# Moving the step sizes and decays of a state-space mixer into the layer ahead of it

## What is computed

```python
proj = h @ w_in                                  # 1024 -> 2048 (z) + 3072 (xbc) + 32 (dt)
xbc = silu(causal_dwconv(xbc, conv_w, conv_b))   # 4 taps
dt = softplus(dt_raw + dt_bias)                  # 32 heads x 256 tokens
a = -exp(a_log)
# ssd_chunked, 2 chunks of 128 tokens, 4 groups of 8 heads, head 64, state 128
a_cs = cumsum(dt * a)                            # inside each chunk
xdt = x * dt
decay = exp(a_cs[l] - a_cs[s]) for s <= l
y_diag = ((C B^T) * decay) @ xdt
states = B^T @ (exp(a_cs[last] - a_cs) * xdt)    # chunk 0 hands its state to chunk 1
y_off  = (C @ states) * exp(a_cs)
y = (y_diag + y_off + x * d_skip) * silu(z)
y = grouped_rms_norm(y) ; out = y @ w_out
```

## Time and profile before

| what | value |
|---|---|
| median of three runs | 1482.74 us (1481.03 to 1485.03) |
| profiled execution, its own time | 1484.64 us |
| its span in the trace | 1482.9 us |
| mean granted clock of TensorE | 0.964 of full speed |
| busy: TensorE, VectorE, ScalarE, GpSimd | 93%, 70%, 51%, 10% of the span |
| TensorE's share of the chain that ended last | 71% |

### The profile page before, as it was taken

One profiled execution on the slowest core, in us unless ns is written; L12 is line 12 of the kernel. 1 busy time (PEld: TensorE's weight loads), 2 busy tenths in 40 slices (PEclk: granted clock), 3 DMA queues, 4 the chain that ended last, 5 costly groups with the idle time before them and its releaser, 6 DMA issues.

```text
span 1482.9 us, 30231 instructions
## 1 busy us (share of the span) xinstructions
PE 1381.3 (93%) x12445; PEld 1325.4 (89%) x12445; DVE 1040.0 (70%) x1688; ACT 761.6 (51%) x1257; POOL 141.5 (10%) x147
## 2 busy tenths in 40 slices
PE   7998999997798999999997599999999998899997
PEld 6997988896798999999995499999999887899997
DVE  5769898986676656557696877887555655678843
ACT  5594483326645444354563855544454455554432
POOL 2000000000101111001002102211010100222100
PEclk9999999997999999999999699999999999999999
DMA  8533510210262665645445344554655521455550
GB/s 267 171 113 114 172 56 2 88 60 30 92 194 86 205 191 165 198 149 160 154 135 153 114 154 158 172 174 148 219 171 175 196 85 59 157 185 170 180 190 29
DMA packets 204338, 211.05 MB, mean 142 GB/s; under 512 B 8579, under 2 KB 201867, under 8 KB 204059
## 3 DMA queue, kind: packets, MB, share of 16 engines
q1 hardware_dynamic: 202154, 200.87, 42.7%
q0 software_dynamic: 1968, 8.44, 2.0%
q10 hardware_dynamic: 96, 0.02, 0.0%
HBM read 207.70 MB, written 1.62 MB: 141 GB/s over the span
## 4 chain that ended last, share of the span: by engine, by line
PE 71%; DVE 16%; ACT 5%; issue 4%; DMA 2%; POOL 1%; SPq 0%; DVEq 0%; ACTq 0%; POOLq 0%
PE pb L417 19%; PE pb L419 19%; PE pb L418 19%; DVE w_lo L446 2%; DVE pj L1453 2%; PE pb L1937 1%; DVE sub L1381 1%; PE pb L403 1%; PE pb L2307 1%; DVE x_lo L1229 1%; PE pb L1979 1%; PE pb L1926 1%; ACT w_hi L440 1%; DVE sub L1382 1%; PE pb L1932 1%
## 5 line engine op out<-in xcount | busy, mean ns | idle before, releaser
L446 DVE TENSOR_TENSOR w_lo<-raw,w_hi 128x1024 fp32r<-128x1024 f32 (+1 forms) x384 | 471.3, 1230 | 161.1 <-ACT w_hi L440 160.5
L417 PE MATMUL pb<-x_hi,w_hi 128*128 128x256 f32 x1968 | 564.2, 287 | 19.8 <-DVE w_lo L446 10.1
L440 ACT ACTIVATE w_hi<-raw 128x1024 fp32r<-128x1024 f32 (+1 forms) x384 | 395.5, 1042 | 340.9 <-PE pb L419 298.9
L418 PE MATMUL pb<-x_lo,w_hi 128*128 128x256 f32 x1968 | 559.9, 284 | 0.0
L419 PE MATMUL pb<-x_hi,w_lo 128*128 128x256 f32 x1968 | 559.8, 284 | 0.0
L417 PEld LDWEIGHTS pb<-x_hi,w_hi 128*128 128x128 f32 x1968 | 381.1, 194 | 24.7 <-DVE w_lo L446 15.9
L418 PEld LDWEIGHTS pb<-x_lo,w_hi 128*128 128x128 f32 x1968 | 381.0, 194 | 0.3
L419 PEld LDWEIGHTS pb<-x_hi,w_lo 128*128 128x128 f32 x1968 | 380.8, 193 | 0.0
L417 PE MATMUL pb<-act_hi,w_hi 128*128 128x256 f32 x528 | 149.5, 283 | 1.1 <-DVE w_lo L446 1.1
L418 PE MATMUL pb<-act_lo,w_hi 128*128 128x256 f32 x528 | 149.4, 283 | 0.0
L419 PE MATMUL pb<-act_hi,w_lo 128*128 128x256 f32 x528 | 149.4, 283 | 0.0
(11 more groups left out here) (312 smaller groups left out, 2103.2 us busy)
## 6 DMA issues: line engine op xcount, KB each, us to landing
raw<-in_ffn_w_up_dram SPq DMA_DIRECT2D x55, 1024.0 KB, 5.1
raw<-in_w_in_dram SPq DMA_DIRECT2D x28, 1024.0 KB, 5.1
raw<-in_ffn_w_down_dram SPq DMA_DIRECT2D x24, 896.0 KB, 4.8
raw<-in_ssd_w_in_dram SPq DMA_DIRECT2D x20, 1024.0 KB, 5.3
raw<-in_fox_w_in_dram SPq DMA_DIRECT2D x16, 1024.0 KB, 5.8
raw<-in_ffn_w_down_dram SPq DMA_DIRECT2D x12, 1024.0 KB, 5.3
raw<-in_ffn_w_gate_dram SPq DMA_DIRECT2D x11, 1024.0 KB, 5.3
raw<-in_ssd_w_out_dram SPq DMA_DIRECT2D x8, 1024.0 KB, 6.3
```

The lines of the kernel that those rows point to most:

```text
L417: pe.matmul(o, w_hi[m][:, k, :], hi[:, k0 + k, :], start=first and k == 0, stop=False)
L418: pe.matmul(o, w_hi[m][:, k, :], lo[:, k0 + k, :], start=False, stop=False)
L440: act.activation(w_hi[m][:, 0:nk, :], raw[s][:, 0:nk, m * P:(m + 1) * P], ACT.Copy).then_inc(sem("w_hi_ready"), 1)
L446: dve.tensor_tensor(w_lo[m][:, 0:nk, :], raw[s][:, 0:nk, m * P:(m + 1) * P], w_hi[m][:, 0:nk, :].bitcast(F32), ALU.subtract).then_inc(sem( ...
```

## The change

- **Step sizes early.** The 32 step-size columns (`dt_w`, 128 KB) are no longer a layer. SyncE loads them ahead of `down0`, after a wait for the last `w_lo` of `up0`. TensorE does `narrow_product` between `ssd_z` and `ssd_xbc`. VectorE and ScalarE do the step sizes and decays behind block (0, 1) of `ssd_xbc`; ScalarE loads the table of Ln and Exp there, and that of SiLU again before the first `xbc_sigmoids`.
- **Decays broadcast early.** GpSimd sends `acs` out at that point and fetches six `att` pieces at once (i = 0 to 5), then writes exp(acs) of chunk 1, 32x128, to DRAM and broadcasts it as `eab`, which now lies in the chunk 1 half of `y_ssd` and needs no exponential afterwards.
- **Scaled x on VectorE.** `xdt_end` is made in four pieces of 128x512 on VectorE, between the pieces of `xdt` of chunk 1, instead of one 128x2048 on GpSimd. It lies where `x_lo` was, and `b_tok` where `x_hi` was.
- **Four units ahead of the states.** Units 0 to 3 run before the chunk states and y_off (`chunk_states`, called at i = `FIRST_UNITS` = 4 on TensorE and VectorE). The skip terms move from i = 0..7 to i = 4..11, the `ssd_out` splits on VectorE from i = 4..6 to i = 9..11; ScalarE's three heads for `ssd_out` move into the last unit of `ssd_xbc`.

The core of the diff:

```diff
+        x_lo_plain = nc.alloc_sbuf_tensor_at("x_lo_plain", [P, KC * T], F32, offset=x_hi_base + KC * T * 4)
+        xdt_end = x_lo_plain[:, :]
+        NATT, FIRST_UNITS = 6, 4
...
+        eab = y_ssd[:, :, P:T]
+        dt_w = pj[:, 90, :].rearrange("p (k n) -> p k n", n=SSD_HEADS)
+        acs_exp = small[:, P:T]
+        b_tok = x_hi_plain[:, 0:512].rearrange("p (g n) -> p g n", g=SSD_GROUPS)
...
-        layer("ssd_dt", narrow(a["ssd_w_in_2"][0], 5120, SSD_HEADS), [KC], dmas=(1, 0))
...
+                if ly.name == "down0":
+                    sp.wait_ge(sem("w_lo_ready"), L["up0"].item1)
+                    sp.dma_start(dt_w, a["ssd_w_in_2"][0].rearrange("(k p) n -> p k n", p=P)[:, :, 5120:5120 + SSD_HEADS]).then_inc(sem("dt_w_loaded"), 16)
...
             pool.wait_ge(sem("sub_dma"), ACS_OUT)
-            pool.wait_ge(sem("xbc_ready"), SSD_XBC)
+            for i in range(NATT):
+                decay_piece(i)
+            pool.wait_ge(sem("da_ready"), 1)
+            pool.dma_start(acs_dram[2], acs_exp).then_inc(sem("sub_dma"), 16)
+            pool.wait_ge(sem("sub_dma"), ACS_OUT + 16)
             for h in range(2):
-                src = acs_dram[1].rearrange("(a m t) l -> t a m l", a=1, t=2)[h]
+                src = acs_dram[2].rearrange("(a m t) l -> t a m l", a=1, t=2)[h]
                 pool.dma_start(eab[64 * h:64 * h + 64, :, :], src.broadcast_to([64, SSD_Z, P])).then_inc(sem("sub_dma"), 16)
-            for i in range(2):
-                decay_piece(i)
-            pool.wait_ge(sem("xdt_ready"), 4)
-            pool.tensor_tensor(xdt_end.rearrange("p (h d) -> p h d", d=HEAD),
-                               xdt[:, 0, :].rearrange("p (h d) -> p h d", d=HEAD),
-                               tok_heads[:, 4, :].unsqueeze(2).broadcast_to([P, SSD_HEADS, HEAD]), ALU.mult).then_inc(sem("xdt_end_ready"), 1)
-            pool.wait_ge(sem("st_done"), SSD_GROUPS)
-            for i in range(2, 16):
-                if i >= NATT:
-                    pool.wait_ge(sem("y_done"), i - NATT + 1)
+            for i in range(NATT, 16):
+                pool.wait_ge(sem("y_done"), i - NATT + 1)
...
+                if isinstance(u, int) and (u, m) == (0, 1):
+                    step_sizes()
+
+            def step_sizes():
+
+                log_exp()
+                act.wait_ge(sem("small_loaded"), 16 * 12)
+                go(act.activation(heads_col[:, 3:4], heads_col[:, 1:2], ACT.Exp))
+                act.wait_ge(sem("abs_ready"), 1)
+                link(act.activation(dt_e, dt_e, ACT.Exp, scale=-1.0))
+                act.activation(dt_e, dt_e, ACT.Ln, bias=1.0).then_inc(sem("log_ready"), 1)
+                act.wait_ge(sem("acs_ready"), 2)
+                act.activation(acs_exp, acs[:, P:T], ACT.Exp)
+                act.activation(da_end, acs[:, 0:P], ACT.Exp, scale=-1.0, bias=acs[:, P - 1:P]).then_inc(sem("da_ready"), 1)
...
-            act_layer(act, L["ssd_xbc"], xbc_hook, lead=2)
+            act_layer(act, L["ssd_xbc"], xbc_hook, lead=2, nxt=L["ssd_out"])
...
-            ahead(act_head, act, L["ssd_out"])
...
-            dve_layer(dve, ly, xbc_block, rest_last=True)
-
-            dve.wait_ge(sem("narrow_done"), 1)
...
+            def step_sizes(u, m):
+
+                if not (isinstance(u, int) and (u, m) == (0, 1)):
+                    return
+                dve.wait_ge(sem("narrow_done"), 1)
+                dve.wait_ge(sem("small_loaded"), 16 * 12)
+                for h in range(2):
+                    go(dve.tensor_copy(d_skip[64 * h:64 * h + 64, :], d_rows[64 * h:64 * h + 64, h::2]))
+                link(tt(dt_z, pb[4][0:SSD_HEADS, 0:T], rstd[0:SSD_HEADS, :], ALU.mult))
...
+            dve_layer(dve, ly, xbc_block, step_sizes, rest_last=True, lead=2)
+            dve.wait_ge(sem("heads_turned"), 1)
...
+                if i >= 4:
+                    dve.wait_ge(sem("xdt_ready"), b + 1)
+                    tt(xdt_end[:, 512 * b:512 * b + 512].rearrange("p (h d) -> p h d", d=HEAD),
+                       xdt[:, 0, 512 * b:512 * b + 512].rearrange("p (h d) -> p h d", d=HEAD),
+                       tok_heads[:, 4, 8 * b:8 * b + 8].unsqueeze(2).broadcast_to([P, 8, HEAD]), ALU.mult).then_inc(sem("xdt_end_ready"), 1)
...
+            def chunk_states():
+
+                for g in range(SSD_GROUPS):
+                    dve.wait_ge(sem("st_done"), g + 1)
+                    dve.tensor_copy(st_ssd[:, 512 * g:512 * g + 512], pb[6 + g % 2][:, :]).then_inc(sem("st_ready"), 1)
+
+                for b in range(4):
+                    dve.wait_ge(sem("yoff_done"), b + 1)
+                    dve.wait_ge(sem("sub_dma"), 96)
+                    tt(y_ssd[:, 4 * b:4 * b + 4, P:T], pb[4 + b % 2][:, :].rearrange("p (m l) -> p m l", l=P),
+                       eab[:, 4 * b:4 * b + 4, :], ALU.mult).then_inc(sem("eab_used"), 1)
+                dve.wait_ge(sem("eab_used"), 4)
...
+                if i == FIRST_UNITS:
+                    chunk_states()
+                if i >= 8:
+                    sync()
...
-                if i < 8:
-                    for m in (2 * i, 2 * i + 1):
+                if FIRST_UNITS <= i < FIRST_UNITS + 8:
+                    for m in (2 * (i - FIRST_UNITS), 2 * (i - FIRST_UNITS) + 1):
                         go(stt(y_ssd[:, m, P:T], xbc[:, m, P:T], d_skip[:, m:m + 1], y_ssd[:, m, P:T], ALU.mult, ALU.add))
-                if i == 8:
-                    sync()
-                if 4 <= i < 4 + LOOKAHEAD:
-                    dve_rest(dve, L["ssd_out"], 0, 0, i - 4)
+                if 9 <= i < 9 + LOOKAHEAD:
+                    dve_rest(dve, L["ssd_out"], 0, 0, i - 9)
...
+            pe.wait_ge(sem("dt_w_loaded"), 16)
+            narrow_product(dt_w, SSD_HEADS, 1)
             pe_layer(pe, L["ssd_xbc"], x_hi, x_lo, "x_lo_ready", X_BASE[2])
-            s = L["ssd_dt"].u0 % 2
-            pe.wait_ge(sem(f"landed{s}0"), L["ssd_dt"].landed[0][0])
-            narrow_product(raw[s], SSD_HEADS, 1)
+            pe.wait_ge(sem("da_ready"), 1)
+            for i, src in enumerate((acs[:, 0:P], acs[:, P:T], dt[:, 0:P], dt[:, P:T], da_end)):
+                ins = turn(pb[4][:, SSD_HEADS * i:SSD_HEADS * i + SSD_HEADS], src)
+            ins.then_inc(sem("heads_turned"), 1)
...
-            pe.wait_ge(sem("heads_ready"), 1)
-            pe.wait_ge(sem("b_tok_ready"), 1)
-
-            pe.wait_ge(sem("xdt_end_ready"), 1)
-            pe.wait_ge(sem("xdt_ready"), 8)
...
+                if i == FIRST_UNITS:
+                    chunk_states()
```

117 lines of the change are left out of this document (40 added, 77 removed).

## The result

| | kernel before | changed kernel |
|---|---|---|
| median | 1481.03 us (5 runs) | 1492.73 us (5 runs, 1489.74 to 1497.0) |
| profiled execution, its own time | 1484.64 us | 1492.31 us |
| its span | 1482.9 us | 1490.5 us |
| mean granted clock | 0.964 | 0.958 |

The ratio is 1.0069, with a 95% interval of 1.0043 to 1.0095: slower, by more than the 0.3% that a measurement of this kernel can tell. The prediction said 1485.2 us, 1479.5 to 1489.0, most likely no difference. It was wrong, and too low.

What follows compares the result with a forecast made beforehand. TensorE was taken to bound `ssd_z` and `ssd_xbc`, with idle engines in the stage behind. Terms 1.3 + 3.6 + 2.4 - 4.8 = +2.5 us on the median of 1482.74 us gave 1485.2 us, range 1479.5 to 1489.0.

Steps and rivals of the forecast that it cites:

- Part 1: Ahead of `down0`: SyncE's wait for the last `w_lo` of `up0` makes `down0` start later, +1.3 us.
- The twin at `down1`: The kernel before's same wait, ahead of `down1`'s small load: 9.38 us from `w_lo` to product, TensorE waiting 1.12 us.
- Part 2: Between `ssd_z` and `ssd_xbc`: the moved `narrow_product` has nothing to cover it there, +3.6 us.
- part 4: From the end of `ssd_xbc` to `ssd_out`: unit 12 begins earlier, four units in the place of GpSimd's product, -4.8 us.
- Part 3: Inside `ssd_xbc`: step sizes on VectorE delay TensorE over blocks (1, 1) and (1, 2), +2.4 us.
- Rival C: In `ssd_xbc`: step sizes stand in full on TensorE's path, 5.3 us in place of 2.4, 1488.1 us; chance 0.18.
- aside on a drain: In `ssd_xbc`: by the skill's 2.66 us per table switch, ScalarE is held 2.8 us longer, the sum 1.9 us higher.
- B: At the chunk states: TensorE's clock stays at 2.4 GHz, 3.3 us less, 1481.9 us; chance 0.16.
- D: Everything goes well: B, a 1.0 us stall in `ssd_xbc`, a tail 1.85 us shorter; 1478.6 us or below; chance 0.10.
- E: Behind `ssd_xbc`: late `att` pieces hold ScalarE, up to 4.8 us of gain lost, 1490.0 us; chance 0.08.
- the sign that the prediction named: In units 9 to 12 behind `ssd_xbc`: ScalarE waiting for `att` pieces would show E; no size given.

Runs made afterwards that it cites:

- the filled wait: The changed kernel with 14 unused products on TensorE ahead of `down0`; 1489.59 us, 1.005 of the kernel before.
- the second product: The kernel before with the step-size product made a second time, result unused, between `ssd_z` and `ssd_xbc`; 1488.42 us, 1.0041 of the kernel before.
- The gap filled: The changed kernel with the `dt_w` load moved to `ssd_z` without its wait, plus 24 unused TensorE products ahead of C B^T; 1487.02 us, ratio 1.0026.
- load unheld: The changed kernel with the `dt_w` load at the same place ahead of `down0`, without SyncE's wait; 1491.94 us, 1.0074 of the kernel before.
- load later: The changed kernel with the `dt_w` load moved from ahead of `down0` to `ssd_z`, without its wait; 1488.37 us, 1.0051 of the kernel before.

## Why the prediction was wrong

**Part 1 was mis-sized: 1.3 us forecast, 3.9 measured.** The mechanism was right and named, the wait in SyncE's queue. The step that failed is "with 9.38 us it starts at 593.94": it was 10.36 us. The twin at `down1` takes 9.38 to 11.31 us over the 14 traces that have its wait (TensorE idle for 1.1 to 3.1), so the one row that I had was the lowest of them. The larger part of the miss, 1.6 us, I had put at nothing: here a wait of 2.10 us was followed by a fall of the clock, while the one of 1.12 us, my model, was not. That the idle time brings the fall is shown by the filled wait, which keeps the layer at 63.46 us.

**Part 2 was right**, 3.6 us, and confirmed by the second product. But "taking it away frees nothing by itself" stopped one step short: it costs something, and that cost falls in part 4. The product covered an idle TensorE, and its going left 3.27 us of idleness.

**Part 3 was right in kind and a little high**, 1.9 us against 2.4. The waits stand where they were forecast, at 739 and 743 in the second unit. Rival C, 5.3 us, is excluded. The prediction's aside on a drain has ScalarE held 2.8 us longer and the stall only 1.9 us longer, without the step between the two; the rows show no drain, so nothing hangs on it.

**Part 4 was mis-sized: -4.8 us forecast, -2.6 measured.** The failed step is its first: "C B^T runs from 789.22 to 791.3 as before". It starts in time, but at half the clock, which puts unit 0 1.9 us and unit 4 2.0 us back. From unit 4 to unit 12 the forecast holds to 0.2 us. The gap filled gives 2.9 us back. The reason that I had for the gain, four units in the place of GpSimd's product, isn't borne out: none against four, and four against six units ahead, give stages within 0.7 us of each other. The -2.6 is itself one pair of traces: the kernel before's stage took 68.03 to 69.44 us in four traces of this code, the changed kernel's 65.87 to 66.95 in seven.

Of the rivals, B is out: TensorE had 3.03 us of idle time ahead of the first unit's products, and the clock was 0.50 from 813 to 819 and 0.53 to 822; only behind 822, at the end of the states, it was 1.00. D asked for B. E's cost is not there: ScalarE does wait 6.6 and 7.6 us for pieces of `att`, ahead of units 6 and 10 (at 818 and 833), which is the sign that the prediction named, but VectorE's units 4 to 12 take the forecast time. So that sign was a poor one: it can be there at no cost.

**What stays open:** the terms make 6.7 us, the medians differ by 10 to 12. Programs with the same local time (load unheld and load later, 265.0) have medians 3.6 us apart. The median of the unheld load, 1.0074 of the kernel before, is no lower than that of the changed kernel, 1.0069, though its trace is 3.9 us better around `down0`. The traces scatter by several us in two places outside the local time; whether the change shifts how often these two places are slow, which could explain the rest, is not shown.

## What to carry to other kernels

Before moving work off a waiting engine, ask what the clock does in the hole that it leaves: here 3.6 us of work moved cost 3.6 us where it went and 2 us where it had been. Price a new wait in a dense stream with what follows it, and take a single row of a like wait as one sample out of several. When medians and terms disagree by a few microseconds, compare fixed marks over two or more executions of each kernel: the local time scattered by at most 1.7 us in unchanged code, while the whole of the kernel before ranged over 11 us (1477.4 to 1488.6 in 30 runs).
